# Opening of a fused encoder layer: the tiles of h rounded by ScalarE straight from x, their full and low parts made by GpSimd

## The reference, cut to what matters

```python
x = _layernorm(x, ln_in_g, ln_in_b)
mod = (silu(c) @ w_ada[l] + b_ada[l]).reshape(B, 3, 3, D)
shift, scale, gate = mod[:, :, 0], mod[:, :, 1], mod[:, :, 2]
h = x * (1.0 + scale[:, 0]) + shift[:, 0]
y = _swiglu(h, ffn1_w_in[l], ffn1_w_out[l])       # silu(h @ Wg) * (h @ Wu) @ Wo
```

## Time and profile before

| | |
|---|---|
| median of 3 runs | 937.65 us (937.12 to 939.71) |
| profiled execution | 938.05 us, span of its core 936.2 us, granted TensorE clock 0.999 |
| TensorE busy | 923.8 us (99%), 4845 matmuls |
| VectorE busy | 600.9 us (64%) |
| ScalarE busy | 422.4 us (45%) |
| GpSimd busy | 275.8 us (29%) |
| chain that ended last | TensorE 95%, DMA 2%, VectorE 1%, ScalarE 1% |

### The profile page before, as it was taken

One profiled execution on the slowest core, in us unless ns is written; L12 is line 12 of the kernel. 1 busy time (PEld: TensorE's weight loads), 2 busy tenths in 40 slices (PEclk: granted clock), 3 DMA queues, 4 the chain that ended last, 5 costly groups with the idle time before them and its releaser, 6 DMA issues.

```text
span 936.2 us, 12697 instructions
## 1 busy us (share of the span) xinstructions
PE 923.8 (99%) x4845; PEld 777.1 (83%) x4845; DVE 600.9 (64%) x875; ACT 422.4 (45%) x673; POOL 275.8 (29%) x239
## 2 busy tenths in 40 slices
PE   8999999999999999999999999999999999999997
PEld 5788888888888888787776677889999999888886
DVE  6956776445454964687775577788777777533334
ACT  6753223332322232483576646655556555322124
POOL 0021111111112522155863655832111111035124
PEclk9999999999999999999999999999999999999999
DMA  9936556656653663324421112196777775623402
GB/s 359 377 113 213 192 186 206 193 180 202 192 180 129 202 227 128 102 68 135 114 67 46 46 51 86 67 258 159 181 192 181 178 193 148 225 79 107 123 18 90
DMA packets 50507, 144.88 MB, mean 155 GB/s; under 512 B 5264, under 2 KB 7440, under 8 KB 50448
## 3 DMA queue, kind: packets, MB, share of 16 engines
q1 hardware_dynamic: 45008, 134.65, 43.0%
q0 software_dynamic: 4896, 8.92, 6.1%
q10 hardware_dynamic: 544, 0.52, 0.2%
HBM read 138.83 MB, written 4.19 MB: 153 GB/s over the span
## 4 chain that ended last, share of the span: by engine, by line
PE 95%; DMA 2%; DVE 1%; SPq 1%; ACT 1%; issue 0%; ACTq 0%; DVEq 0%
PE bank L890 23%; PE bank L892 23%; PE bank L891 23%; PE bank L1001 6%; PE bank L1003 6%; PE bank L1002 6%; PE bank L1304 2%; DMA raw<-wunits 1%; PE bank L1328 1%; DMA ada_first<-ada_w 1%; PE bank L1315 1%; PE bank L1068 1%; PE bank L975 1%; PE bank L976 1%; PE bank L969 0%
## 5 line engine op out<-in xcount | busy, mean ns | idle before, releaser
L1431 DVE TENSOR_TENSOR w_lo<-raw,w_hi 128x1024 fp32r<-128x1024 f32 (+1 forms) x117 | 160.7, 1383 | 132.1 <-ACT w_hi L1403 131.7
L890 PE MATMUL bank<-h_hi,w_hi 128*128 128x512 f32 x455 | 178.9, 393 | 0.0
L892 PE MATMUL bank<-h_hi,w_lo 128*128 128x512 f32 x455 | 177.4, 390 | 0.0
L891 PE MATMUL bank<-h_lo,w_hi 128*128 128x512 f32 x455 | 177.3, 390 | 0.0
L1403 ACT ACTIVATE w_hi<-raw 128x1024 fp32r<-128x1024 f32 (+1 forms) x118 | 118.7, 1023 | 116.5 <-PE bank L892 111.6
L890 PE MATMUL bank<-a_hi,w_hi 128*128 128x512 f32 (+1 forms) x338 | 128.3, 379 | 0.0
L891 PE MATMUL bank<-a_lo,w_hi 128*128 128x512 f32 (+1 forms) x338 | 127.9, 378 | 0.0
L892 PE MATMUL bank<-a_hi,w_lo 128*128 128x512 f32 (+1 forms) x338 | 127.8, 378 | 0.0
L2539 POOL TENSOR_TENSOR a_lo<-act_t,a_hi 128x512 fp32r<-128x512 f32 x27 | 37.7, 1395 | 251.5 <-ACT a_hi L1526 251.4
L892 PEld LDWEIGHTS bank<-h_hi,w_lo 128*128 128x128 f32 x455 | 85.5, 188 | 18.0
L890 PEld LDWEIGHTS bank<-h_hi,w_hi 128*128 128x128 f32 x455 | 85.5, 188 | 17.9 <-issue 0.5
(11 more groups left out here) (374 smaller groups left out, 1949.2 us busy)
## 6 DMA issues: line engine op xcount, KB each, us to landing
raw<-wunits SPq DMA_DIRECT2D x110, 512.0 KB, 3.5
ada_ring<-ada_w SPq DMA_DIRECT2D x56, 512.0 KB, 4.4
raw_ab<-wunits SPq DMA_DIRECT2D x18, 512.0 KB, 4.7
ada_first<-ada_w SPq DMA_DIRECT2D x16, 512.0 KB, 11.6
raw<-wunits SPq DMA_DIRECT2D x32, 256.0 KB, 3.8
raw<-wunits POOLq DMA_DIRECT2D x32, 256.0 KB, 4.8
raw<-wunits SPq DMA_DIRECT2D x16, 384.0 KB, 2.9
raw_d<-wunits SPq DMA_DIRECT2D x17, 256.0 KB, 2.7
```

Source lines behind the costliest of these rows:

```text
L890: mm(out, lh, rh, start=first, stop=False)
L891: mm(out, lh, rl, start=False, stop=False)
L892: return mm(out, ll, rh, start=False, stop=last)
L1431: nc.vector.tensor_tensor(lo, raw_of(n, width), hi.bitcast(F32), SUB).then_inc(s_lo, 1)
```

## The change

ScalarE makes `h_hi[k]` (k = 1 to 7) in one instruction from `x[k]` with scale and bias. The full-precision tile `act_t` is made by GpSimd (a `tensor_scalar` on `x[k]` with the same two columns), and GpSimd also makes all eight `h_lo[k]` (a `tensor_tensor`). VectorE's `first_low` is gone. The bias copies stay ahead of the new loop on GpSimd; `ffn(0, 1)`, with the first `a_split`, comes behind it.

```diff
@@ ScalarE, for k = 1 to 7
                     act.wait_ge(s_fc, k + 1)
                     act.wait_ge(s_tfree, k + 1)
-                    if k >= 2:
-                        act.wait_ge(s_hl[0], k - 1)
-                    fn(act_t[:, k % 2, :], x[:, k, :], ACT.Identity, scale=first_col[:, k, 0:1],
-                       bias=first_col[:, k, 1:2]).then_inc(s_hf[0], 1)
-                    act.wait_ge(s_hf[0], k + 1)
-                    fn(h_hi[:, k, :], act_t[:, k % 2, :], ACT.Copy).then_inc(s_hh[0], 1)
+                    fn(h_hi[:, k, :], x[:, k, :], ACT.Identity, scale=first_col[:, k, 0:1],
+                       bias=first_col[:, k, 1:2]).then_inc(s_hh[0], 1)
@@ VectorE
-            def first_low(k):
-
-                dve.wait_ge(s_hh[0], k + 1)
-                dve.wait_ge(s_hf[0], k + 1)
-                tt(h_lo[:, k, :], act_t[:, k % 2, :], h_hi[:, k, :].bitcast(F32), SUB).then_inc(s_hl[0], 1)
-
...
-                if k:
-                    first_low(k - 1)
                 for n in range(2) if k == 0 else range(k + 1, min(k + 2, EARLY)):
                     dve_lo(dve, n)
-            first_low(KD - 1)
@@ GpSimd, behind the two bias copies
+            for k in range(KD):
+                if k:
+                    pool.wait_ge(s_fc, k + 1)
+                    pool.wait_ge(s_tfree, k + 1)
+                    if k >= 2:
+                        pool.wait_ge(s_hl[0], k - 1)
+                    ts(act_t[:, k % 2, :], x[:, k, :], first_col[:, k, 0:1], first_col[:, k, 1:2], MUL, ADD)\
+                        .then_inc(s_hf[0], 1)
+                pool.wait_ge(s_hh[0], k + 1)
+                pool.wait_ge(s_hf[0], k + 1)
+                tt(h_lo[:, k, :], act_t[:, k % 2, :], h_hi[:, k, :].bitcast(F32), SUB).then_inc(s_hl[0], 1)
             ffn(0, 1)
```

## The result

| | before | after |
|---|---|---|
| median | 937.68 us (6 runs, 937.12 to 939.71) | 941.75 us (6 runs, 940.24 to 942.63) |
| ratio after / before | | 1.004, 95% interval 1.003 to 1.0051 |
| profiled execution | 938.05 us, span 936.2 | 940.24 us, span 938.2 |

The change costs 4.1 us, 0.4%: more than the 0.3% that tells a loss from no change here, though the interval begins at that bound. The forecast was a loss of 1.9 us, called no change; the time lies within its range, 0.4 us from the upper end. The profiled execution is the lowest of the six and shows 2.2 us of the 4.1. Of these 0.2 lie outside the span (2.04 us of time beyond it, 1.85 before).

What follows compares the result with a forecast made beforehand. TensorE was taken as the bound, with the opening up to line 975 for k = 3 movable. The shift of 1.76 plus 0.15 for `h_lo[7]`, +1.9 us on 937.65, gave 939.6 us, range 938.0 to 942.2.

Steps and rivals of the forecast that it cites:

- What bounds, and the way to the end: TensorE bounds; line 975 for k = 3, at 33.64 us, sets all that follows, its shift carried one for one.
- ScalarE's 0.66 us: ScalarE in the opening: one instruction instead of two makes `h_hi` 0.66 us earlier for the same start.
- The price of a GpSimd subtraction: VectorE in the opening: each GpSimd subtraction costs it 2.31 - 1.22 = 1.09 us, as both wait for each other.
- The estimate of 1.41 us a turn: VectorE's cost per turn by the skill's text, 1.29 + 0.115 us; would add 0.96 us, left out.
- They take turns: Opening: VectorE and GpSimd alternate at 1.09 and 0.64 us, columns of k = 3 at 34.50, line 975 +1.76 us.
- 0.64 us: VectorE in the opening: cost of each GpSimd `tensor_scalar`, from an op of 1.38 us against 0.74 alone.
- Rival 2: Opening: GpSimd's one-input op is passed over by VectorE ops; line 975 for k = 3 +2.8 us, 940.5; chance 0.22.
- rival 3: Opening: GpSimd pushed out for whole steps, or TensorE's clock falls in a 1.5 us hole; 944; chance 0.08.
- the 0.15: End of the opening: `h_lo[7]` comes at 56.15 us, TensorE wants it at 56.02; 0.15 us added.
- The mechanism called most likely: Opening: VectorE and GpSimd taking turns, own range 938.6 to 940.8 us, chance 0.58.

Runs made afterwards that it cites:

- one pair: Changed kernel with one pair of throw-away TensorE matmuls in each of two holes, ahead of tile 1's high part and its low part: 940.75 us, ratio 1.003.
- low part only: Changed kernel with ScalarE as in the kernel before (full tile, then its rounding) and GpSimd making only the low parts: 939.01 us, ratio 1.0011.

## Why the prediction was right and wrong

- **What bounds, and the way to the end:** right in the main. The start of line 975 for k = 3 set the opening, and its shift reached the end of the span one for one (0.2 us more lie outside the span). What it stood behind was the low part `h_lo[2]`, not `h_hi[3]` as forecast.
- **ScalarE's 0.66 us:** near (0.53 in the stretch when tried by itself).
- **The price of a GpSimd subtraction, 1.09 us of VectorE's time:** right (columns at 33.21 for 33.22; a column sum of 2.29 us in the changed kernel). The estimate of 1.41 us a turn would have put these columns near 34.2; its 115 ns are told in the Trainium skill of a DMA's descriptors that wait for VectorE, not of this pair.
- **"They take turns", for the `tensor_scalar`:** this step failed. I gave it 0.64 us and a turn behind the op at work; it stood through that op and one or two more (2.80 and 3.78 us). Rival 2 (chance 0.22) is in the main what happened: `act_t[1]` at 27.5 (rival: 28.0), `h_lo[1]` at 29.8 (30.2), columns of k = 3 at 32.6 (where the forecast had 34.5), line 975 at 35.94 (36.5), and the last wait for `h_lo[2]`. The row that told it, 2.79 us in the earlier trace rows, stood in the argument; I weighed it as one row against many of another form.
- **The clock:** put into rival 3 with 0.08 as something no row shows. It did fall, 0.2 us after a hole of 1.4 us (the longest before was 1.1), and about 1.0 us of the median's loss goes with it.
- **`h_lo[7]`:** no wait at line 992 in the changed kernel, as VectorE ended sooner; the 0.15 was not paid.
- **The size:** 1.9 forecast, 4.1 measured: 2.4 of waits in the opening, about 1.0 of clock, 0.2 outside the span, and 0.3 to 0.5 that the traces don't show. This rest **stays open**, and so does why the 0.2 appear (in every kernel in which GpSimd makes both tiles, in none of the others). The profiled executions of the changed kernel's first measurement and of the two with throw-away matmuls are each the lowest of their runs.
- **Luck:** that the time fell inside the range is owed to its width, which held rival 2 as well. The mechanism called most likely (0.58) had 940.8 as its own upper end, and about 1.0 us of the loss is a fall of the clock that stood only in rival 3.

## What to carry to other kernels

An idle GpSimd is no free engine beside a VectorE whose queue is full of ops with two SBUF inputs: count each of its two-input ops at nearly its own length on VectorE, and assume that a one-input op stands through the op at work and one or two behind it. When a step is moved off a critical engine, look for the row where both engines already had a queue and use the one of the same form, even where it is a single one. A hole that a change opens ahead of TensorE can cost its clock besides its length, so look at the granted clock behind it.

## What the runs showed of the hardware

- A one-input `tensor_scalar` of GpSimd (0.77 us alone) stood still for three VectorE ops with two SBUF inputs in a row (3.78 us), a two-input op of the same size for one (1.95 us, 1.04 alone), from the same place in the order. In another run it got in between two such ops that stood in line (3.26 us). The Trainium skill (SBUF — State Buffer, "Who interferes with whom") says that the order of issue, not the shape of the op, decides who blocks. For the two-input op the trace agrees; for the one-input op it does not, and the measurement decides.
- The same section says that a VectorE instruction with at most one SBUF input doesn't contend outside the 2-port modes. The trace agrees: sums that read PSUM took 1.22 us beside a GpSimd subtraction of 1.28.
- TensorE's granted clock stood at 0.50, the 1.2 GHz level, for 3.4 us in three profiles: from 24.7 to 28.1 in the changed kernel, 0.2 us after a hole of 1.41; from 30.9 to 34.3 in its second profile, 0.9 us after a hole of 2.54; from 25.0 to 28.4 with ScalarE direct and GpSimd's low part, 0.3 us after a hole of 1.41. It stayed at 1.00 over holes of 1.13 (before), 1.40 (two-input op), 1.69 (one pair) and 2.06 (low part only). So the length of a hole alone doesn't tell; what does stays open.
